# A second transformer mixer rearranged: half of its output projection among the last attention blocks, the first gate and value units early, the normalisation in pieces

## The chip, the cores and the metric

The kernel runs on one core of one Trainium2 chip. The metric is the device time of one execution in microseconds (us), lower is better. The core's engines are TensorE (PE in the profile, with its weight loads as PEld), VectorE (DVE), ScalarE (ACT), GpSimd (POOL) and SyncE (SP); each runs its own instruction list in order, and they wait for each other by semaphores.

## What is computed

Two networks of two layers each run one after the other on 512 tokens of width 1024. The change lies in the mixer of the second network, which runs once in each of its layers, between two feed-forward blocks. Cut to what matters:

```python
def hybrid_mixer(x, w_in, sc_conv_w, attn_sink, cc_conv_w, cc_conv_b, cc_ln_g, cc_ln_b, w_out):
    z = x @ w_in
    sc_b, sc_c, sc_h, q, k, v, cc_a, cc_gate = jnp.split(z, IN_OFFSETS, axis=-1)
    y_sc = sc_b * depthwise_conv(sc_c * sc_h, sc_conv_w)                      # 3 taps, 256 channels
    q, k = rope(q), rope(k)                                                   # 8 query heads, 2 key heads
    y_att = banded_window_attention(q, k, v, attn_sink)                       # blocks of 128, width 512
    u = depthwise_conv(cc_a * jax.nn.sigmoid(cc_gate), cc_conv_w) + cc_conv_b # 31 taps, 256 channels
    y_cc = jax.nn.silu(layer_norm(u, cc_ln_g, cc_ln_b))
    return jnp.concatenate([y_sc, y_att, y_cc], axis=-1) @ w_out

x = layer_norm(ALPHA * x + hybrid_mixer(x, ...), ln2_g, ln2_b)   # then the second feed-forward block
```

## The kernel before

One Python class stands for each engine (`TensorE`, `VectorE`, `ScalarE`, `Pool`, `Sync`) and writes that engine's whole instruction list. The classes walk through the same stages with the same generators, so the order on each engine is written out by hand; a `wait_ge` on a key waits for the instruction of another engine that announced the key.

**Precision.** A product of two fp32 matrices is made of three matmuls (`three`): high part by high part, high by low, low by high. Each weight unit is a 128x1024 fp32 tile. SP loads it to `raw` (three slots), ScalarE casts it to the high part `whi` (L2010), and VectorE subtracts to get the low part `wlo` (L1147). `whi` and `wlo` have four slots (`RING`), and a slot is free again when TensorE has announced `used` for the unit in it. `take()` and `ahead()` say where in the lists of ScalarE and VectorE the split of a coming unit stands; `spend(i)` marks a slot that may be taken.

**The mixer.** TensorE first makes the queries (four units, all held), then keys and values (`kv`, two units held, 96 matmuls of 256 columns). VectorE turns them with `rope_q` and `rope_k`, TensorE transposes them, ScalarE copies the transposes. Then come two interleaved streams. The main one, `attention`, goes through eight blocks (`BLOCKS`: four query blocks by two key heads): `scores` (four steps, a 256 or 384 column matmul each; VectorE adds the mask and finds the maximum; ScalarE's `weights` takes the exponential), then, for the block before, `values` (five steps: transposes of the weights on TensorE, ScalarE's copy `prT`, matmuls with `v` at L1134, and VectorE's scaling `ao`), then one empty step. That makes 80 steps. After every second block a transpose of the heads' outputs, `turn_ao`, is copied to `xh8` (ScalarE) and its low part to `xl8` (VectorE).

The other stream, `beside`, has 80 side steps of three 512-column matmuls, 8 steps to a unit: gate, value, gate, value (`conv_units`, for the 31-tap convolution), then two times three units for the 3-tap one (`short_conv`). Next to it stands `wide_conv`: on VectorE the 60 taps of the 31-tap convolution, one instruction of 512 columns each (two more instructions start the halves); on TensorE the two means of its normalisation, in banks of `ps`. A counter in `beside` sets its pace: no tap before side step 17, then four taps in three side steps up to tap 60, then one piece of the normalisation each fourth side step; `drain(wide)` runs what is left. `mix(..., 76, 74)` puts the two streams together, almost one to one, after six side steps. The end of the normalisation, one instruction list on VectorE (reciprocal at L1933, scaling, low part) and on ScalarE (`Silu`, cast), stands inside the last third of the stream.

After both streams `project` makes the output projection: two column halves, each four units (`w_out`) by four token tiles. For half 0 the units go one after another, for half 1 all four are held and the tiles follow each other (`late` is 1 and 4). VectorE adds the residual (`xn`, L1153) and does the layer norm tile by tile; TensorE transposes the first two tiles (`to_hT_tile`) inside half 1. Half 0 uses PSUM banks 4 to 7 and half 1 banks 0 to 3; the next feed-forward block begins with four units in banks 0 to 3.

**PSUM banks.** Eight banks, in rotations: `ps` is 4 to 7 (scores, transposes), `main2` is 0 and 1 (`kv`, `ao`), `side2` is 2 and 3 (side units). `bank()` waits until the last user of the bank is done.

Of the kernel before, what the change touches and what calls it, by code (L numbers as in the profile page):

```python
# [516 lines left out]
class TensorE(Lane):  # L517
    serial = False

    def __init__(self, k, e, name):  # L520
        super().__init__(k, e, name)
        self.all4, self.ps = Rota([0, 1, 2, 3]), Rota([4, 5, 6, 7])
        self.main2, self.side2 = Rota([0, 1]), Rota([2, 3])
        self.side3, self.adas = Rota([0, 1, 2]), Rota([3])
        self.pool3, self.small3 = Rota([2, 3, 7]), Rota([4, 5, 6])
# [67 lines left out]
    def tiles(self, keys, name, index, k0s, col, xh, xl, ready, rota, late):  # L593


        banks = [self.bank(rota, key) for key in keys]
        nk, held = 2 * len(k0s), []
        for ui, k0 in enumerate(k0s):
            held.append((ui,) + self.coming(name, index, n_pieces(k0, col)))
            if 0 <= len(k0s) - late <= ui < len(k0s) - 1:  # L600
                continue
            if ui == len(k0s) - 1:
                order = [(h, j, t) for t in range(4) for h in held for j in range(2)]
            else:
                order = [(h, j, t) for h in held for j in range(2) for t in range(4)]
            for q, ((u, wh, wl, i), j, t) in enumerate(order):
                k = 2 * u + j
                x = slice(k * 512 + t * 128, k * 512 + (t + 1) * 128)
                self.wait_ge(("hi", i), ("lo", i), *ready(k))
# [10 lines left out]
    def to_hT_tile(self, st, t):  # L620
        k = self.k
        self.wait_ge(("x", st, t), ("ident",))
        x = k.xs if st[0] == "A" else k.xn
        for d4 in range(2):
            bank = self.bank(self.ps, ("hT", st, t, d4))
            self.turn(bank, [x[:, t * 1024 + d * 128:t * 1024 + (d + 1) * 128] for d in range(4 * d4, 4 * d4 + 4)],
                      ("hT", st, t, d4))
# [374 lines left out]
    def mixer(self, l):  # L1002
# [5 lines left out]
        for t in range(4):  # L1008
            bank = self.bank(self.all4, ("q", l, t))
            for u, (wh, wl, i) in enumerate(units):  # L1010
                self.wait_ge(("hi", i), ("lo", i), ("hh", st, t, u // 2), ("hl", st, t, u // 2))
                for j in range(2):
                    d = 2 * u + j
                    x = slice(512 * d + 128 * t, 512 * d + 128 * t + 128)
                    a = self.three(bank[:, :], k.hh[:, x], k.hl[:, x], HALF(wh, j), HALF(wl, j), d == 0, d == 7)
                a.then_inc(*self.up(*([("used", i)] if t == 3 else []), *([("q", l, t)] if u == 3 else [])))
            if t < 2:
                self.to_hT_tile(st, 2 + t)
            else:
                self.turn_q(l, t - 2)  # L1020
        units = [self.coming("w_in_2", (l,), tuple((512 * u + 128 * j, 1280, 256) for j in range(4))) for u in range(2)]
        for t in range(4):
# [10 lines left out]
            if t % 2:  # L1033
                self.turn_q(l, 2 + t // 2)
        side = self.beside(l, 1)
# [4 lines left out]
        mix(self.attention(l), side, 76, 74)  # L1040
        drain(side)
        self.project("w_out_2", l, [0, 256, 512, 768], k.xh8, k.xl8, lambda d: (("xh", l, d), ("xl", l, d)), st, ("ffn2", l))
# [13 lines left out]
    def conv_units(self, l):  # L1056
        for j in range(2):
            yield from self.proj2(("cgt", l, j), l, 1792 + j * 128, self.side2)
            yield from self.proj2(("ca", l, j), l, 1536 + j * 128, self.side2)
        yield from self.short_conv(l)  # L1060
# [7 lines left out]
    def wide_conv(self, l):  # L1068
# [3 lines left out]
        bank = self.bank(self.ps, ("cm", l))  # L1072
# [5 lines left out]
        bank = self.bank(self.ps, ("cv", l))  # L1078
# [6 lines left out]
    def attention(self, l):  # L1085
        held = None
        for at in BLOCKS:
            yield from self.scores(l, *at)
            if held:
                yield from self.values(l, *held)  # L1090
            held = at
            yield
        yield from self.values(l, *held)
        self.turn_ao(l, 3)

    def turn_ao(self, l, nb):
        k = self.k
        bank = self.bank(self.ps, ("aot", l, nb))
        self.wait_ge(("aon", l, nb, 1))
        self.turn(bank, [k.ao[:, i * 128:(i + 1) * 128] for i in range(4)], ("aot", l, nb))  # L1100

    def scores(self, l, nb, kvh, k0, nk):
        k = self.k
        for i in range(4):
            h, q = 4 * kvh + i, 64 * kvh
            bank = self.bank(self.ps, ("as", l, nb, h))
# [7 lines left out]
    def values(self, l, nb, kvh, k0, nk):  # L1114
# [3 lines left out]
        out = self.bank(self.main2, ("ao", at))  # L1118

        def turned(i):  # L1120
            bank = self.bank(self.ps, ("at", at, i))
# [21 lines left out]
class VectorE(Lane):  # L1143
    at_steps = (2, 6)

# [628 lines left out]
    def project(self, n, st, nxt, s, ln, eps):  # L1774
        k = self.k
        self.at(("pj", st))
        stat = k.stat
        for half in range(2):
            late = (1, 4)[half]
            for ui in range(n):  # L1780
# [4 lines left out]
            for t in range(4):  # L1785
                if half and t == 2 and nxt != ("ffn1", DEPTH):
                    self.turn(nxt, 0)
                if t == 3:
                    self.spend(first + 1 if half else first)
# [32 lines left out]
    def mixer(self, l):  # L1822
# [12 lines left out]
        self.rope_q(l, 3)  # L1835
        used = [self.take() for _ in range(2)]
        self.rope_k(l, 0)
        for i in used:
            self.spend(i)
            self.ahead()  # L1840
# [4 lines left out]
        mix(self.attention(l), side, 76, 74)  # L1845
        drain(side)
        self.project(4, st, ("ffn2", l), ALPHA, "ln2", 1e-5)
# [31 lines left out]
    def conv_units(self, l):  # L1879
        k = self.k  # L1880
        z = [x[:, :] for x in k.t3]
        cp = k.ccp[:, :].rearrange("p (j n) -> p j n", j=2)
        for j in range(2):
            yield from self.steps()
            yield from self.steps()
            self.wait_ge(("cgs", l, j), ("ca", l, j), ("pads", l))
            self.tt(cp[:, j, 15:527], k.bank(("ca", l, j))[:, :], z[0], ALU.mult).then_inc(
                *self.up(("cuu", l, j), ("free", ("ca", l, j))))
        yield from self.short_conv(l)

    def short_conv(self, l):
# [3 lines left out]
        for j in range(2):  # L1895
            yield from self.steps()
# [4 lines left out]
            self.wait_ge()  # L1901
            self.ts(z[1], sp[:, j, 0:512], k.col(("sc", l, 0), j), None, ALU.mult).then_inc(*self.up())
            for w in (1, 2):
                self.wait_ge()
                self.stt(z[1], sp[:, j, w:w + 512], k.col(("sc", l, w), j), z[1], ALU.mult, ALU.add).then_inc(*self.up())
            yield from self.steps()
            self.wait_ge(("sc", l, j, 2))
            self.tt(z[1], z[1], k.bank(("sc", l, j, 2))[:, :], ALU.mult).then_inc(*self.up(("scy", l, j), ("free", ("sc", l, j, 2))))
            self.lower(HALF(k.xl8, j), z[1], HALF(k.xh8, j), [("xh", l, j)], [("xl", l, j)])

    def wide_conv(self, l):
# [21 lines left out]
        self.e.reciprocal(z[:, 0:512], z[:, 0:512]).then_inc(*self.up())  # L1933
        for j in range(2):
# [3 lines left out]
            self.lower(HALF(k.xl8, 6 + j), ac, HALF(k.xh8, 6 + j), [("xh", l, 6 + j)], [("xl", l, 6 + j)])  # L1938
# [62 lines left out]
class ScalarE(Lane):  # L2001
    at_steps = (0, 4)

# [353 lines left out]
    def project(self, n, st, nxt):  # L2357
        self.at(("pj", st))
        for half in range(2):
# [12 lines left out]
    def mixer(self, l):  # L2372
# [11 lines left out]
        for i in used[2:]:  # L2384
            self.spend(i)
            self.ahead()
        used = [self.take() for _ in range(2)]
        self.turned_q(l, 2)
# [4 lines left out]
        self.turned_q(l, 3)  # L2393
        self.value(l, 1)
        side = self.beside(l)
# [4 lines left out]
        mix(self.attention(l), side, 76, 74)  # L2400
        drain(side)
        self.project(4, st, ("ffn2", l))
# [21 lines left out]
    def conv_units(self, l):  # L2424
        k = self.k
        z = [x[:, :] for x in k.t3]
        for j in range(2):
            yield from self.steps()
            key = ("cgt", l, j)
            self.wait_ge(key, *([("cuu", l, 0)] if j else []))  # L2430
            self.act(z[0], k.bank(key)[:, :], ACT.Sigmoid).then_inc(*self.up(("cgs", l, j), ("free", key)))
            yield from self.steps()
        yield from self.short_conv(l)
# [14 lines left out]
    def wide_conv(self, l):  # L2448
# [10 lines left out]
        for j in range(2):  # L2459
# [4 lines left out]
            self.e.copy(HALF(k.xh8, 6 + j), ac).then_inc(*self.up(("xh", l, 6 + j)))  # L2464

# [333 lines left out]
```

## Time and profile before

| | us |
|---|---|
| median of 3 runs | 3529.51 (3528.66 to 3537.89) |
| the profiled execution, its own time | 3529.57 |
| its span, first to last instruction | 3527.7 |
| TensorE busy | 3347.5 (95%) |
| VectorE busy | 1724.9 (49%) |
| ScalarE busy | 1102.4 (31%) |
| mean granted TensorE clock | 0.975 |

The span is 1.9 us shorter than the execution's own time. Busy time of TensorE counts overlapping matmuls once; a matmul's end is modelled, so its start-to-start distance says more than its duration. The two mixers lie at about 1920 to 2175 us and 2920 to 3155 us of the span.

### The profile page before, as it was taken

The page shows a single profiled execution, that of the slowest core. Times are in us where ns is not written, and L with a number is a line of the kernel's source. Part 1 is how long each engine was busy: PE and PEld are TensorE (multiplying, and loading weights), DVE is VectorE, ACT ScalarE, POOL GpSimd, SP SyncE. Part 2 cuts the span into 40 slices and gives each one's busy share as a digit, 9 for nine tenths or more (in the row PEclk, how much of TensorE's full clock was granted, in tenths as well). Part 3 has the DMA queues.
Part 4 walks back from the last instruction along what each step waited for, and adds up shares of the span by engine and source line. Part 5 has one row for each costly group of instructions (what it writes and reads, how often), then busy time and mean ns, then how long its engine had stood idle before and what let it go on. Part 6 is the DMA issues. An engine that isn't in the chain of part 4 may idle for free. (4 is left out here: it accounts for less than half of the span.)

```text
span 3527.7 us, 42459 instructions
## 1 busy us (share of the span) xinstructions
PE 3347.5 (95%) x16776; PEld 2733.4 (77%) x16776; DVE 1724.9 (49%) x2524; ACT 1102.4 (31%) x1619; POOL 146.6 (4%) x204
## 2 busy tenths in 40 slices
PE   6999899989999999999999989999999999889999
PEld 5777777867777778788887758888888886578887
DVE  6655654456545544453334675332533346753334
ACT  4342223224432232233322443332233224323321
POOL 1000000001000000000001001000000000010000
PEclk9999999999999999999999989999999999899999
DMA  5222122132221111223232202223222322113232
GB/s 222 72 88 92 66 66 78 60 111 96 84 78 66 60 43 55 84 82 103 97 112 85 72 30 79 101 96 114 84 97 100 108 78 84 36 66 102 98 111 78
DMA packets 83494, 303.13 MB, mean 86 GB/s; under 512 B 9680, under 2 KB 9952, under 8 KB 83296
## 3 DMA queue, kind: packets, MB, share of 16 engines
q1 hardware_dynamic: 78064, 283.11, 23.5%
q0 software_dynamic: 5232, 17.31, 1.5%
q8 instruction: 133, 2.18, 0.2%
q14 instruction: 65, 0.53, 0.0%
HBM read 295.66 MB, written 4.72 MB: 85 GB/s over the span
## 5 line engine op out<-in xcount | busy, mean ns | idle before, releaser
L554 PE MATMUL bank<-hh,whi 128*128 128x512 f32 (+1 forms) x2704 | 1081.1, 400 | 25.0 <-DVE xn L1153 9.5
L556 PE MATMUL bank<-hh,wlo 128*128 128x512 f32 (+1 forms) x2704 | 1035.1, 383 | 0.0
L555 PE MATMUL bank<-hl,whi 128*128 128x512 f32 (+1 forms) x2704 | 1033.4, 382 | 0.0
L1147 DVE TENSOR_TENSOR wlo<-raw,whi 128x1024 fp32r<-128x1024 f32 x498 | 610.5, 1226 | 784.6 <-ACT whi L2010 722.6
L2010 ACT CAST whi<-raw 128x1024 fp32r<-128x1024 f32 x498 | 523.6, 1051 | 754.6 <-PE bank L556 696.4
L554 PEld LDWEIGHTS bank<-hh,whi 128*128 128x128 f32 x2704 | 520.0, 192 | 156.3 <-issue 46.6
L556 PEld LDWEIGHTS bank<-hh,wlo 128*128 128x128 f32 x2704 | 518.4, 192 | 98.7
L555 PEld LDWEIGHTS bank<-hl,whi 128*128 128x128 f32 x2704 | 520.6, 193 | 80.7 <-issue 2.7
L554 PE MATMUL bank<-whi,fh 128*128 128x512 f32 x704 | 274.4, 390 | 0.0
L556 PE MATMUL bank<-whi,fl 128*128 128x512 f32 x704 | 273.9, 389 | 0.0
L555 PE MATMUL bank<-wlo,fh 128*128 128x512 f32 x704 | 273.9, 389 | 0.0
L1147 DVE TENSOR_TENSOR tmp<-tmp,bank 128x512 f32<-128x512 f32 x104 | 71.5, 688 | 243.2 <-PE bank L556 240.9
L2354 ACT CAST fh<-tmp 128x512 fp32r<-128x512 f32 x88 | 54.5, 619 | 375.3 <-DVE tmp L1147 375.3
L555 PEld LDWEIGHTS bank<-wlo,fh 128*128 128x128 f32 x704 | 132.2, 188 | 27.3
L556 PEld LDWEIGHTS bank<-whi,fl 128*128 128x128 f32 x704 | 132.2, 188 | 27.3
L554 PEld LDWEIGHTS bank<-whi,fh 128*128 128x128 f32 x704 | 132.2, 188 | 27.3
L872 PEld LDWEIGHTS bank<-X,G 128*128 128x128 f32 x768 | 100.3, 195 | 27.9 <-ACT X L2273 14.0
L872 PEld LDWEIGHTS bank<-U,Y 128*128 128x128 f32 x768 | 100.1, 194 | 15.3 <-ACT Y L2277 8.6
L872 PE MATMUL bank<-X,G 128*128 128x64 f32 x768 | 101.0, 275 | 10.0 <-ACT X L2273 9.8
L1625 DVE COPY_PREDICATED U<-lmask,bank 128x256 f32<-128x256 uint32 x64 | 32.7, 510 | 149.3 <-PE bank L872 148.9
L872 PE MATMUL bank<-U,Y 128*128 128x64 f32 x768 | 98.9, 272 | 1.9 <-ACT Y L2277 1.9
L1147 DVE TENSOR_TENSOR fl<-tmp,fh 128x512 fp32r<-128x512 f32 x88 | 61.0, 693 | 71.6 <-ACT fh L2354 71.6
(320 smaller groups left out, 3707.8 us busy)
## 6 DMA issues: line engine op xcount, KB each, us to landing
raw<-in_W SPq DMA_DIRECT2D x514, 512.0 KB, 3.3
bc<-in_ln_g POOLq DMA_DIRECT2D x6, 512.0 KB, 4.3
bc<-in_ln_b POOLq DMA_DIRECT2D x6, 512.0 KB, 5.7
xn<-in_x SPq DMA_DIRECT2D x4, 512.0 KB, 8.9
mrg<-in_W SPq DMA_DIRECT2D x2, 1024.0 KB, 12.9
AR<-in_W SPq DMA_DIRECT2D x2, 1024.0 KB, 18.0
xn<-in_x POOLq DMA_DIRECT2D x4, 512.0 KB, 5.3
xd<-xn POOLq DMA_DIRECT2D x4, 512.0 KB, 3.5
```

The source lines that it names most:

```text
L554: e.matmul(out, ah, bh, start=first, stop=False, skip_group_check=True)
L555: e.matmul(out, ah, bl, start=False, stop=False, skip_group_check=True)
L556: return e.matmul(out, al, bh, start=False, stop=last, skip_group_check=True)
L872: t = self.e.matmul(bank[:, i * 64:(i + 1) * 64], lhs(i), rhs(i), start=True, stop=True, skip_group_check=True)
L1147: return self.e.tensor_tensor(o, a, b, op)
L1625: e.copy_predicated(FOUR_PART(U, 1, n), m, TIGHT(wb, n)).then_inc(*self.up(("cu", at, lv + 1), ("free", ("cw", at, lv))))
L2010: self.e.copy(self.k.halves(i)[0], self.k.raw_unit(n)).then_inc(*self.up(("hi", i)))
L2354: self.e.copy(HALF(k.fh, m), tm).then_inc(*self.up(("fh", st, m)))
```

## The change

1. The first gate and value units (`conv_pair(l, 0)`) come before `kv`. The first 10 taps run on VectorE around `rope_k(0)`, before `beside`.
2. In `beside` taps run one to a side step up to tap 60 at side step 50; each engine then has its own list of side steps at which it does a piece of the normalisation (`norm_steps`). The reciprocal is cut into two halves, and the scaling and the low part into separate pieces.
3. `out_half` makes half 0 of the output projection as 32 more side steps, in the row order `OUT_ROWS`: short convolution, wide convolution, then the two units of attention held together, tile by tile. With the 16 steps moved ahead the side stream has 96; `mix(..., 80, 78)` puts 78 beside attention after six, and 12 follow it.
4. PSUM banks: `ao` has bank 0 alone, the means bank 1, scores and transposes three banks (4, 5, 6) from the seventh block on; half 0 goes to 1, 7, 2, 3 and half 1 to 0, 4, 5, 6; the transposes of the first two tiles after it to 7, 1, 2, 3.
5. In `short_conv` the three tap instructions are spread over the unit's steps, and the low part is taken later (`low_short`).
6. `project` skips half 0's units; the mark `("pj", st)`, after which POOL loads the gain and bias rows of the layer norm (`bc`), stands before the mix.

```diff
+OUT_ROWS = (0, 768, 256, 512)
...
-    def beside(self, l, early=0):
-        wide = self.wide_conv(l)
-        done = 0
-        for n, _ in enumerate(self.conv_units(l), 1):
-            m = n + early
-            while done < min(60, (m - 17) * 4 // 3) + max(0, (m - 62) // 4):
-                next(wide, None)
-                done += 1
-            yield
-        drain(wide)
+    def taps(self, n):
+        for _ in range(n):
+            next(self.wide, None)
+    def beside(self, l):
+        done = 10
+        for m, _ in enumerate(itertools.chain(self.conv_units(l), self.out_half(l)), 1):
+            want = min(10 + m, 60) + sum(m >= x for x in self.norm_steps)
+            self.taps(want - done)
+            done = max(done, want)
+            yield
...
+    norm_steps = (52, 58)                     # TensorE
+    norm_steps = (54, 60, 63, 64, 66, 71)     # VectorE
+    norm_steps = (55, 61, 68)                 # ScalarE
...
+        self.ao1, self.ps3, self.norm1 = Rota([0]), Rota([4, 5, 6]), Rota([1])
+        self.first4, self.last4, self.spare4 = Rota([1, 7, 2, 3]), Rota([0, 4, 5, 6]), Rota([7, 1, 2, 3])
...
+    def out_half(self, l):                    # TensorE
+        k, st = self.k, ("mix", l)
+        self.mark(("hlast", ("ffn2", l)))
+        units, banks = [], []
+        for u, k0 in enumerate(OUT_ROWS):
+            units.append(self.coming("w_out_2", (l,), n_pieces(k0, 0)))
+            if u == 2:
+                continue
+            held = range(2, 4) if u == 3 else (u,)
+            order = [(t, v, j) for t in range(4) for v in held for j in range(2)]
+            for t, v, j in order if u == 3 else [(t, u, j) for j in range(2) for t in range(4)]:
+                wh, wl, i = units[v]
+                d = OUT_ROWS[v] // 128 + j
+                if v == j == 0:
+                    banks.append(self.bank(self.first4, ("pj", st, 0, t)))
+                x = slice(512 * d + 128 * t, 512 * d + 128 * t + 128)
+                self.wait_ge(("hi", i), ("lo", i), *([("xah", l, t), ("free", ("aot", l, t))] if u == 3 else [("xh", l, d), ("xl", l, d)]))
+                a = self.three(banks[t][:, :], k.xh8[:, x], k.xl8[:, x], HALF(wh, j), HALF(wl, j), v == j == 0, v == 3 and j == 1)
...
+                yield
...
         self.rope_q(l, 3)                     # VectorE, mixer
+        drain(self.conv_pair(l, 0))
+        self.wide = self.wide_conv(l)
+        self.taps(5)
         used = [self.take() for _ in range(2)]
         self.rope_k(l, 0)
+        self.taps(5)
...
-        self.e.reciprocal(z[:, 0:512], z[:, 0:512]).then_inc(*self.up())
+        self.e.reciprocal(z[:, 0:256], z[:, 0:256]).then_inc(*self.up())
+        yield
+        self.e.reciprocal(z[:, 256:512], z[:, 256:512]).then_inc(*self.up())
+        yield
...
-        mix(self.attention(l), side, 76, 74)
+        self.at(("pj", st))
+        mix(self.attention(l), side, 80, 78)
         drain(side)
-        self.project(4, st, ("ffn2", l), ALPHA, "ln2", 1e-5)
+        self.project(4, st, ("ffn2", l), ALPHA, "ln2", 1e-5, self.held)
```

## Rows read from the trace of the kernel before

**Rows 1.** The page: TensorE's line, and the two groups that split weight units.

```profile
PE 3347.5 (95%) x16776; PEld 2733.4 (77%) x16776; DVE 1724.9 (49%) x2524; ACT 1102.4 (31%) x1619; POOL 146.6 (4%) x204
...
L1147 DVE TENSOR_TENSOR wlo<-raw,whi 128x1024 fp32r<-128x1024 f32 x498 | 610.5, 1226 | 784.6 <-ACT whi L2010 722.6
L2010 ACT CAST whi<-raw 128x1024 fp32r<-128x1024 f32 x498 | 523.6, 1051 | 754.6 <-PE bank L556 696.4
```

**Rows 2.** Busy time by stretches: length, engines' busy (instructions), clock, DMA share, GB/s.

```profile
1960.71:2148.70 187.99, 164.61 (x777) 120.65 (x776) 121.30 (x234) 76.61 (x151) 1.06 (x2) 0.91 0.18 59
2940.32:3128.30 187.98, 164.65 (x777) 120.66 (x776) 121.29 (x234) 76.63 (x151) 1.06 (x2) 0.91 0.17 59
2940.32:2953.05 12.73, 12.73 (x109) 12.72 (x108) 6.42 (x12) 4.78 (x7) 0.00 (x0) 1.00 0.47 162
2953.05:2958.03 4.98, 4.84 (x26) 3.77 (x24) 3.62 (x6) 2.36 (x5) 0.00 (x0) 1.00 0.55 166
2976.00:3060.20 84.20, 76.20 (x326) 51.53 (x325) 73.86 (x139) 32.91 (x72) 0.00 (x0) 0.90 0.11 38
3078.70:3091.00 12.30, 0.03 (x2) 0.01 (x1) 7.68 (x10) 4.94 (x8) 0.00 (x0) 0.59 0.12 43
3091.00:3106.46 15.46, 13.05 (x64) 10.92 (x64) 3.21 (x11) 7.06 (x18) 0.00 (x0) 0.77 0.00 1
3106.46:3128.30 21.84, 21.84 (x96) 18.11 (x97) 8.75 (x10) 4.84 (x5) 1.06 (x2) 1.00 0.44 143
```

**Rows 3.** TensorE's waits, 2930 to 3170: us in total, times, longest.

```profile
PE bank L1134 <- ACT prT L2511: 13.3, 3, 12.3
PE bank L560 <- DVE sm L1968: 3.3, 2, 2.8
```

**Rows 4.** VectorE's groups from 2976.00 to 3060.20, shapes apart.

```profile
L1153 DVE SCALAR_TENSOR_TENSOR acc<-ccp,cols,acc 128x512 f32<-128x512 f32 x60 | 45.1, 752 | 2.1
...
L1984 DVE RECIPROCAL sm<-sm 128x4 f32<-128x4 f32 x5 | 0.9, 178 | 0.2
```

**Rows 5.** Timeline of the normalisation's end: start, duration, engine, line, operation, idle before.

```profile
3079.99 3.35 DVE L1933 RECIPROCAL zc<-zc 128x512 f32<-128x512 f32 x1
...
3084.21 1.28 ACT L2005 ACT_TABLE_LOAD   x1 [8.90 <-DVE acc L1153]
3085.51 0.72 ACT L2005 ACTIVATE acc<-acc,cols 128x512 f32<-128x512 f32 x1
...
3090.03 0.69 DVE L1147 TENSOR_TENSOR xl<-acc,xh 128x512 fp32r<-128x512 f32 x1 [1.57 <-ACT xh L2464]
...
3091.00 0.48 PE L1134 MATMUL bank<-v,prT 128*128 128x64 f32 x1 [12.27 <-ACT prT L2511]
```

**Rows 6.** Timeline, TensorE: starts of scores, side steps beside values, and a mean.

```profile
2958.03 0.67 PE L1108 MATMUL bank<-kT,qT 64*128 64x256 f32 x2
...
2959.53 0.70 PE L1108 MATMUL bank<-kT,qT 64*128 64x256 f32 x2
...
3012.98 0.48 PE L554 MATMUL bank<-hh,whi 128*128 128x512 f32 x1
...
3014.34 0.48 PE L554 MATMUL bank<-hh,whi 128*128 128x512 f32 x1
...
3015.91 0.91 PE L1108 MATMUL bank<-kT,qT 64*128 64x384 f32 x2
...
3017.64 0.91 PE L1108 MATMUL bank<-kT,qT 64*128 64x384 f32 x2
...
3060.70 1.98 PE L1075 MATMUL bank<-acc,mean 128*128 128x512 f32 x4 [0.80 <-DVE sm L1968]
```

**Rows 7.** Timeline of the seam to the next feed-forward block.

```profile
3149.06 1.42 DVE L1147 TENSOR_TENSOR hl<-bank,hh 128x512 fp32r<-128x512 f32 x2
...
3150.56 1.23 DVE L1147 TENSOR_TENSOR wlo<-raw,whi 128x1024 fp32r<-128x1024 f32 x1
...
3155.25 0.36 PE L554 MATMUL bank<-hh,whi 128*128 128x256 f32 x1 [3.18 <-DVE xn L1153]
```

More of the change, by code:

```diff
@@ L1032, in mixer @@
                 a.then_inc(*self.up(*([("used", i)] if t == 3 else []), *([("kv", l, t // 2)] if u and t % 2 else [])))
-            if t % 2:
-                self.turn_q(l, 2 + t // 2)
-        side = self.beside(l, 1)
+        self.wide = self.wide_conv(l)
+        self.taps(10)
+        side = self.beside(l)
         for n in range(6):
@@ L1039, in mixer @@
                 self.turn_k(l, n // 3)
-        mix(self.attention(l), side, 76, 74)
+        self.at(("pj", st))
+        mix(self.attention(l), side, 80, 78)
         drain(side)
-        self.project("w_out_2", l, [0, 256, 512, 768], k.xh8, k.xl8, lambda d: (("xh", l, d), ("xl", l, d)), st, ("ffn2", l))
+        keys = [("pj", st, 1, t) for t in range(4)]
+        for n, _ in enumerate(self.tiles(keys, "w_out_2", (l,), OUT_ROWS, 512, k.xh8, k.xl8, lambda d: (), self.last4, 4)):
+            if n in (9, 11):
+                self.to_hT_tile(("ffn2", l), n // 11, self.spare4)
+        self.all4.n = 0
+    def out_half(self, l):
[16 more added lines that the diff above has]
+                a = self.three(banks[t][:, :], k.xh8[:, x], k.xl8[:, x], HALF(wh, j), HALF(wl, j), v == j == 0, v == 3 and j == 1)
+                done = [("pj", st, 0, t)] if v == 3 and j else []
+                if t == 3 and j:
+                    done.append(("used", i))
+                if done:
+                    a.then_inc(*self.up(*done))
+                yield
     def turn_q(self, l, t):
@@ L1054, in turn_k, with conv_pair @@
         self.turn(bank, [k.kn[a][:, n * 128:(n + 1) * 128] for n in range(2)], ("kt", l, a))
[L1056 to L1060, printed above, removed]
+    def conv_pair(self, l, j):
+        yield from self.proj2(("cgt", l, j), l, 1792 + j * 128, self.side2)
+        yield from self.proj2(("ca", l, j), l, 1536 + j * 128, self.side2)
     def short_conv(self, l):
@@ L1071, in wide_conv @@
             yield
-        bank = self.bank(self.ps, ("cm", l))
+        bank = self.bank(self.norm1, ("cm", l))
         self.wait_ge(("acc", l), ("mean", l))
@@ L1077, in wide_conv @@
         yield
-        bank = self.bank(self.ps, ("cv", l))
+        bank = self.bank(self.norm1, ("cv", l))
         self.wait_ge(("csq", l))
@@ L1086, in attention @@
         held = None
-        for at in BLOCKS:
+        self.rows_rota = self.ps
+        for n, at in enumerate(BLOCKS):
+            if n == 6:
+                self.rows_rota = self.ps3
             yield from self.scores(l, *at)
@@ L1097, in turn_ao @@
         k = self.k
-        bank = self.bank(self.ps, ("aot", l, nb))
+        bank = self.bank(self.rows_rota, ("aot", l, nb))
         self.wait_ge(("aon", l, nb, 1))
@@ L1117, in values @@
         n0 = 4 * (2 * nb + kvh)
-        out = self.bank(self.main2, ("ao", at))
+        out = self.bank(self.ao1, ("ao", at))
         def turned(i):
-            bank = self.bank(self.ps, ("at", at, i))
+            bank = self.bank(self.rows_rota, ("at", at, i))
             self.wait_ge(("ap", at, i), ("ident",))
@@ L1772, in ffn, with project @@
         self.project(11, st, nxt, 2 * ALPHA, ln, eps)
-    def project(self, n, st, nxt, s, ln, eps):
+    def project(self, n, st, nxt, s, ln, eps, held=()):
         k = self.k
-        self.at(("pj", st))
+        if not held:
+            self.at(("pj", st))
         stat = k.stat
@@ L1779, in project @@
             late = (1, 4)[half]
-            for ui in range(n):
+            for ui in range(0 if held and not half else n):
                 i = self.take()
@@ L1788, in project @@
                 if t == 3:
-                    self.spend(first + 1 if half else first)
+                    for i in (first + 1,) if half else held or (first,):
+                        self.spend(i)
                     self.ahead()
@@ L1844, in mixer @@
             next(side)
-        mix(self.attention(l), side, 76, 74)
+        self.at(("pj", st))
+        mix(self.attention(l), side, 80, 78)
         drain(side)
-        self.project(4, st, ("ffn2", l), ALPHA, "ln2", 1e-5)
+        self.project(4, st, ("ffn2", l), ALPHA, "ln2", 1e-5, self.held)
     def turned_by(self, o, tm, x, cs, sn):
@@ L1877, in rope_k, with conv_pair, out_half @@
         self.tt(o, o, tm, ALU.add).then_inc(*self.up(("kn", l, a)))
-    def conv_units(self, l):
+    def conv_pair(self, l, j):
         k = self.k
-        z = [x[:, :] for x in k.t3]
         cp = k.ccp[:, :].rearrange("p (j n) -> p j n", j=2)
[L1883 to L1889, printed above, removed]
+        yield from self.steps()
+        yield from self.steps()
+        self.wait_ge(("cgs", l, j), ("ca", l, j), ("pads", l))
+        self.tt(cp[:, j, 15:527], k.bank(("ca", l, j))[:, :], k.t3[0][:, :], ALU.mult).then_inc(
+            *self.up(("cuu", l, j), ("free", ("ca", l, j))))
+    def out_half(self, l):
+        for n, _ in enumerate(self.steps(), 1):
+            if n == 2:
+                self.low_short(l, 1)
+            yield
+        yield from self.steps()
+        self.held = self.take(), self.take()
+        for _ in range(16):
+            yield
     def short_conv(self, l):
@@ L1895, in short_conv @@
         for j in range(2):
-            yield from self.steps()
+            for n, _ in enumerate(self.steps(), 1):
+                if j and n == 2:
+                    self.low_short(l, 0)
+                yield
             yield from self.steps()
@@ L1937, in wide_conv @@
             self.stt(ac, ac, k.col(("cc_lg", l), j), z[:, 0:512], ALU.mult, ALU.mult).then_inc(*self.up(("ccn", l, j)))
-            self.lower(HALF(k.xl8, 6 + j), ac, HALF(k.xh8, 6 + j), [("xh", l, 6 + j)], [("xl", l, 6 + j)])
+        yield
+        for j in range(2):
+            self.lower(HALF(k.xl8, 6 + j), HALF(k.acc, j), HALF(k.xh8, 6 + j), [("xh", l, 6 + j)], [("xl", l, 6 + j)])
     def attention(self, l):
@@ L2355, in ffn, with project @@
         self.project(11, st, nxt)
-    def project(self, n, st, nxt):
-        self.at(("pj", st))
-        for half in range(2):
+    def project(self, n, st, nxt, held=()):
+        if not held:
+            self.at(("pj", st))
+        for i in held:
+            self.spend(i)
+        for half in range(1 if held else 0, 2):
             late = (1, 4)[half]
@@ L2386, in mixer @@
             self.ahead()
+        for n, _ in enumerate(self.conv_pair(l, 0), 1):
+            if n == 9:
+                self.turned_q(l, 2)
+        self.turned_q(l, 3)
         used = [self.take() for _ in range(2)]
-        self.turned_q(l, 2)
         self.value(l, 0)
@@ L2392, in mixer @@
             self.ahead()
-        self.turned_q(l, 3)
         self.value(l, 1)
+        self.wide = self.wide_conv(l)
+        self.taps(10)
         side = self.beside(l)
@@ L2399, in mixer @@
                 self.turned_k(l, n // 3)
-        mix(self.attention(l), side, 76, 74)
+        self.at(("pj", st))
+        mix(self.attention(l), side, 80, 78)
         drain(side)
-        self.project(4, st, ("ffn2", l))
+        self.project(4, st, ("ffn2", l), self.held)
     def turned_q(self, l, t):
@@ L2422, in value, with conv_pair, out_half @@
                     k.bank(key)[:, :].rearrange("p (t c n) -> p t c n", t=2, c=2)[:, :, 1, :]).then_inc(*self.up(("vv", l, a), ("free", key)))
-    def conv_units(self, l):
+    def conv_pair(self, l, j):
         k = self.k
[L2426 to L2433, printed above, removed]
+        key = ("cgt", l, j)
+        yield from self.steps()
+        self.wait_ge(key, *([("cuu", l, 0)] if j else []))
+        self.act(k.t3[0][:, :], k.bank(key)[:, :], ACT.Sigmoid).then_inc(*self.up(("cgs", l, j), ("free", key)))
+        yield from self.steps()
+    def out_half(self, l):
+        yield from self.steps()
+        yield from self.steps()
+        self.held = self.take(), self.take()
+        for _ in range(16):
+            yield
     def short_conv(self, l):
@@ L2464, in wide_conv @@
             self.e.copy(HALF(k.xh8, 6 + j), ac).then_inc(*self.up(("xh", l, 6 + j)))
+        yield
     def attention(self, l):
```

35 lines of the change are left out of this document (24 added, 11 removed).

## The prediction

> **What bounds the kernel now.** I read the page first: TensorE is busy 95% of the span [rows 1], so over the whole kernel only its waits and its slow clock can be won, unless work is removed, and the change removes none. Next, the busy time by stretches around the two mixers. From the transposes before `kv` to the end of output half 0 takes 187.98 us, and 187.99 us in the first mixer [rows 2], so what holds for one counts twice. TensorE is busy only 164.65 us of these, at a clock of 0.91: this is the weakest place in the kernel, and the reader should see two causes in its parts.
>
> First, from 2976.00 to 3060.20, while the 60 taps run, VectorE is busy 73.86 of 84.20 us in 139 instructions; between them is a small gap each, so it is nearly full, and it sets the pace. TensorE waits for it in places (3.3 us for score banks, 2.8 the longest) [rows 3] and its clock is 0.90. Second, from 3078.70 to 3091.00 TensorE does nothing at all. The wait list names `prT`, 12.3 us at once [rows 3]; the timeline shows why the copy is late: ScalarE and VectorE stand in the end of the normalisation (reciprocal 3.35 us, `Silu` after an idle 8.90 us, last low part at 3090.03), and the copy is behind it in ScalarE's list [rows 5]. The clock in this stretch is 0.59 and in the 15.46 us after it 0.77 [rows 2], where 1 is the 2.4 GHz level and 0.5 the 1.2 GHz level: of those 15.46 us, 46% ran at half clock, so about 3.6 us were lost besides the wait.
>
> **The change, summed for one mixer.** I lay the new order out from the same start (2940.32) to the start of half 1.
>
> (a) Gate and value units of pair 0, 48 matmuls. Half 0 gives the price: 96 matmuls in 21.84 us [rows 2], 0.228 each, so 11.0 us. A side step of three is 0.68.
>
> (b) `kv` and its transposes, as now: 12.7 us [rows 2].
>
> (c) Six side steps and the key transposes, as now 5.0 us [rows 2]. New in VectorE's list ahead of `rope_k(1)` are 10 taps (7.5 us) [rows 4]; TensorE's `turn_k(1)`, and everything behind it, waits for `rope_k(1)`. Counting the list from the end of (a) (convolution input, five taps, a unit's low part at 1.23 [rows 1], `rope_k(0)`, five taps, two low parts, `rope_k(1)`), I get about 17.5 us, against 16.3 for TensorE: 1.4 us of new wait with the semaphore.
>
> (d) Side steps 7 to 50, with 50 taps instead of 60. By TensorE: 8 scores of 256 columns at 1.50 a step and 12 of 384 at 1.73 [rows 6], together 32.8; value steps at 1.36 for three key blocks [rows 6] and an estimated 1.13 for two (two thirds of what is over 0.68), 8 each, 19.9; 44 transposes, 6.0 (from (b): 12.73 less 96 matmuls at half of 0.228, over the 13 other instructions, 0.14 each [rows 2]); 8 steps without any of these, 5.5. Sum 64. By VectorE: today's 84.20 less 11 instructions at 0.75 [rows 4] is 75.9, less one step of its other work, 0.9: 75. The larger one decides, so I take 75; 64 is the lower bound. The upper bound is today's 84.
>
> (e) Side steps 51 to 84. VectorE has no taps left here, so I count TensorE: 4 scores at 1.73 and 8 at 1.50, 18.9; value steps 8 at 1.36 and 8 at 1.13, 19.9; 48 transposes 6.6; 6 bare steps 4.1; two means at 1.98 or less [rows 6], 3.8. Sum 53. For small waits, as [rows 3] has them outside the longest ones (1.0 and 0.5 us), I add 2; lower bound 0, upper bound the long wait and slow clock of today, which is a rival below.
>
> (f) The last 12 side steps, 8.2 us, with the last `turn_ao` 0.5 and its wait for `ao`, as now about 0.6. They cover the copy and the low part of the last attention tile, which only the last three matmul steps need. Sum 9.2.
>
> Together 11.0 + 12.7 + 6.4 + 75 + 55 + 9.2 = 169.3, against 187.98: **18.7 us less**. Put the other way: 12.3 of the wait and 3.6 of slow clock go, and the rest comes from VectorE's stage and the seam into the projection.
>
> (g) After half 1, TensorE's first feed-forward matmul waits 3.18 us for the residual addition of tile 3, because that frees the fourth bank [rows 7]. With the new banks those four are freed by the transposes' readers instead, done at 3150.48 (3149.06 + 1.42) [rows 7]. What is late next is the first unit's low part at 3151.79 (3150.56 + 1.23) [rows 7], just when half 1 ends. Gain 3.2, lower bound 0 if a later unit waits anyway.
>
> **Costed at nothing.** The split reciprocal: a four-column one takes 0.18 [rows 4] and the whole 3.35 [rows 5], so two halves cost 3.35 plus about 0.18; it lies in (e), where VectorE has room (without taps it had 73.86 less 45.1, 28.8 us, in the 45 steps of the tap stage [rows 2, 4]). If that cover were gone, 0.2 us. The early `bc` loads move 1 MB while the DMA share is 0.17 [rows 2]; if they collided, three raw slots stand between. Half 1 needs all four units in a tile's order, and the splits of its last two cannot begin before the held units are used: cast 1.05 and subtraction 1.23 [rows 1] end about 1.3 and 2.6 us after half 0, and TensorE asks for them 2.7 and 4.1 us after it. Without that cover each would cost its 1.05 to 2.3 us. One bank for `ao`: TensorE's `values` waits until VectorE has scaled the block before; five or six steps lie between, except before the last block, where one empty step of 0.68 stands against 0.42 and a semaphore. Three row banks: at a step of 1.5 us each is read before its turn.
>
> **A rule beside the rows.** In [rows 5] the switch of ScalarE's function table takes 1.28 us and the `Silu` starts 0.02 later. The Trainium skill (ScalarE: Activation LUTs, "What ACT_TABLE_LOAD costs") adds a drain of about 1.38 us to each switch, 2.66 in all, which speaks against putting `Silu` between two exponentials: an estimate by that page adds 2.8 us a mixer for two switches: nothing if hidden, otherwise 3491.4 instead of 3485.8. The rows go against the drain, so I keep 1.28.
>
> **Total.** (18.7 + 3.2) x 2 = 43.8 us. The profiled execution took 3529.57 (span 3527.7 and 1.9 around it), the median is 3529.51. 3529.6 - 43.8 = **3485.8**, some 1.2% less.
>
> **Rivals.**
> *TensorE sets the pace everywhere* (VectorE's 256-column scores in the first blocks are cheaper than those of today's stage, and the clock stays full). (d) is 64 and no wait is added: 154.4, 36.8 less with the seam, 3456. Against it: VectorE has 73.86 less 8.3, 65.6 busy us, and the gaps between some 130 instructions.
> *VectorE's stage doesn't shrink*: in-order waits eat what ten taps free, (d) stays 84: 3485.8 + 18 = 3504. For it: of the 84.20 now 10.3 are gaps and waits [rows 2].
> *The chain is only moved.* TensorE now wants both low parts of the wide convolution at side step 73, VectorE gives them at 71 and ScalarE's `Silu` comes at 68; from the reciprocal at 63 there are ten steps, some 15 us, while today this end lasts 10.7 (3079.99 to 3090.72) [rows 5]. If ScalarE is late by its exponentials, wait and slow clock come back: 15.9 x 2 more, 3518.
> *Slower: the single bank 0.* Every `values` would wait for VectorE's `ao` of the block before, which stands behind taps and low parts in its list. Seven waits in each mixer; from 3.1 us each (43.8/14) the gain is gone; at 5 us each the time is 3556. Against it: with one bank more, TensorE's longest waits today are for others [rows 3], and VectorE has five steps of time.
> *It does nothing on balance*: smaller waits eat it, 3530.
>
> **Chances.** Forecast 0.52 (own range 3475 to 3497); TensorE everywhere 0.14; stage not shrunk 0.16; chain moved 0.10; slower 0.04; nothing 0.04. The range 3456 to 3516 leaves out half of the second case, half of the chain's, and the last two: some 0.2. A measurement here tells about 0.3%, 10.6 us, from no change. Faster by more: the first three cases and most of the fourth, 0.90; within: the rest of the fourth and most of the last, 0.06; slower 0.04.
>
> **What would show it.** No TensorE wait above 3 us in either mixer. From the transposes before `kv` to the first half 1 matmul about 169 us. The tap stage about 75 us with VectorE nearly full, the 34 steps after it some 55 with TensorE full at clock 1.0. The reciprocal as two instructions of about 1.8. The first feed-forward matmul right behind half 1. The prediction is wrong if TensorE waits at the first `out_half` steps of unit 768 (for `xl`), at L1134 before the last block, or if VectorE shows idle time in the tap stage while TensorE waits too.

## The result and the profile after

The changed kernel takes 3490.13 us (median of 4 runs, 3487.3 to 3499.98) against 3529.33 for the kernel before (4 runs): ratio 0.9886, 95% interval 0.9867 to 0.9905, 39 us less. I had forecast 3486 in a range of 3456 to 3516. In a later session the same kernel took 3486.99 against 3529.84 (0.9881, 0.9864 to 0.9899).

The page after: TensorE's line and the span (compare [rows 1]; TensorE does the same 16776 matmuls).

```profile
span 3485.5 us, 42457 instructions
...
PE 3327.7 (95%) x16776; PEld 2715.6 (78%) x16776; DVE 1725.2 (49%) x2526; ACT 1098.4 (32%) x1615; POOL 146.8 (4%) x204
```

Busy time by stretches in the second mixer: from the transposes ahead of the first pair to the first matmul of half 1; the tap stage (first score to last tap); from there to the last `turn_ao`; and two parts of the latter. Columns as in [rows 2].

```profile
2917.86:3090.56 172.70, 159.86 (x777) 116.65 (x776) 121.88 (x236) 74.15 (x149) 1.06 (x2) 0.96 0.18 61
2948.59:3024.30 75.71, 71.62 (x306) 47.34 (x306) 65.79 (x131) 32.01 (x74) 1.06 (x2) 0.93 0.17 57
3024.30:3081.87 57.57, 50.55 (x253) 36.68 (x253) 29.08 (x66) 29.31 (x59) 0.00 (x0) 0.97 0.11 38
3062.90:3067.69 4.79, 0.34 (x3) 0.10 (x2) 2.86 (x8) 2.44 (x6) 0.00 (x0) 1.00 0.15 44
3067.69:3081.87 14.18, 13.59 (x76) 11.92 (x77) 2.73 (x7) 6.28 (x17) 0.00 (x0) 0.88 0.14 49
```

The first line answers to the second of [rows 2]: the same 777 matmuls, 172.70 us in place of 187.98, and the clock 0.96 in place of 0.91. The tap stage is 75.71, with 65.79 busy in 131 instructions on VectorE. The fourth line is what stayed wrong: 4.8 us with next to nothing on TensorE.

TensorE's waits, 2900 to 3170 (compare [rows 3]).

```profile
PE bank L570 <- DVE xl L1194: 6.1, 3, 4.5
PE bank L1180 <- ACT prT L2600: 2.3, 3, 1.3
PE bank L570 <- DVE sm L2042: 1.9, 1, 1.9
PE bank L564 <- DVE qn L1194: 1.1, 1, 1.1
```

The 12.3 us of [rows 3] are gone, and so is the 3.2 at the seam. Two waits are new: 4.5 us for a low part (`xl`) and 1.1 for the rotated queries (`qn`). (`sm` are VectorE's small values for the softmax, maxima and sums; the score bank is free when VectorE has read it for them.) Timeline around the first:

```profile
3055.23 1.28 ACT L2080 ACT_TABLE_LOAD   x1 [1.93 <-DVE acc L1200]
...
3059.33 1.28 ACT L2080 ACT_TABLE_LOAD   x1
...
3060.13 0.66 PE L570 MATMUL bank<-ident,ao 128*128 128x128 f32 x4
...
3063.45 1.04 ACT L2085 CAST whi<-raw 128x1024 fp32r<-128x1024 f32 x1
3064.52 0.59 ACT L2575 CAST xh<-bank 128x512 fp32r<-128x512 f32 x1
3064.62 1.23 DVE L1194 TENSOR_TENSOR wlo<-raw,whi 128x1024 fp32r<-128x1024 f32 x1 [3.58 <-ACT whi L2085]
...
3066.94 0.69 DVE L1194 TENSOR_TENSOR xl<-bank,xh 128x512 fp32r<-128x512 f32 x1
3067.69 0.41 PE L570 MATMUL bank<-ident,pr 128*128 128x128 f32 x1 [4.45 <-DVE xl L1194]
```

Read it from the end. TensorE wants a bank for a transpose of attention weights. With three banks in turn, the next one is that of `turn_ao`, written at 3060.13 and read last at 3067.63. ScalarE's copy of it comes only at 3064.52, because in ScalarE's list it stands behind the normalisation's `Silu`, two table switches, four exponentials and a weight cast. VectorE adds its part: it idles 3.58 us for that weight cast, then makes the weight's low part, a mask and three small values for the softmax first, and so reads the bank (`xl`, 3066.94) only 1.83 us after ScalarE's copy is done (3065.11).

The seam to the feed-forward block, timeline (compare [rows 7]): it starts right behind half 1's last matmul.

```profile
3113.89 0.39 PE L566 MATMUL bank<-whi,xl 128*128 128x512 f32 x1
...
3114.16 0.36 PE L564 MATMUL bank<-hh,whi 128*128 128x256 f32 x1
```

### The profile page after: what moved, and what is told of

Its sections match the earlier page's. It is cut to its first block and busy times, and to the rows that moved or that the text cites. A ratio compares the mean times of both kernels' runs of the same rounds, so it can differ in the third digit from the quotient of the medians.

```text
span 3485.5 us, 42457 instructions
## 1 busy us (share of the span) xinstructions
PE 3327.7 (95%) x16776; PEld 2715.6 (78%) x16776; DVE 1725.2 (49%) x2526; ACT 1098.4 (32%) x1615; POOL 146.8 (4%) x204
```

## Experiments

Whole times of one kernel differ by up to 0.5% between runs, and part of that lies where no edit is (last section). So beside the medians I give the length of the mixer, read the same way from every timeline: start of the second query tile's transposes to the first feed-forward matmul. It is 214.9 us before in both mixers. Tap stage means first score to last tap, from start to start.

| kernel | median us (runs) | ratio to before, 95% | mixers, us | tap stages, us |
|---|---|---|---|---|
| before | 3529.33 (4) | | 214.9, 214.9 | 101.4, 101.4 |
| changed | 3490.13 (4) | 0.9886, 0.9867 to 0.9905 | 196.6, 196.3 | 74.0, 74.9 |
| changed, again | 3486.99 (4) | 0.9881, 0.9864 to 0.9899 | 197.4, 194.6 | 75.6, 72.2 |
| half 0 back | 3518.33 (9) | 0.9960, 0.9944 to 0.9976 | 208.2, 210.6 | 74.0, 75.5 |
| seam banks | 3517.17 (10) | 0.9954, 0.9938 to 0.9971 | 205.9, 204.8 | 75.6, 74.9 |
| no early taps | 3507.19 (4) | 0.9930, 0.9907 to 0.9953 | 204.2, 206.1 | 82.5, 83.4 |
| chain whole | 3497.74 (4) | 0.9900, 0.9876 to 0.9924 | 200.4, 199.5 | 75.6, 74.8 |
| tile 3 in bank 0 | 3503.55 (4) | 0.9920, 0.9900 to 0.9939 | 199.9, 199.4 | 74.0, 73.8 |
| Silu later | 3486.48 (4) | 0.9882, 0.9866 to 0.9898 | 194.3, 192.2 | 74.0, 73.8 |
| no switch | 3478.0 (1) | | 193.1, 189.4 | 74.0, 72.2 |
| fewer taps | 3474.74 (1) | | 189.2, 188.9 | 66.5, 66.4 |
| Silu later, pair in banks 0 and 1 | 3482.21 (4) | 0.9868, 0.9853 to 0.9883 | 192.6, 192.7 | 74.1, 74.2 |
| the same, slower taps | 3486.74 (4) | 0.9869, 0.9853 to 0.9884 | 193.9, 192.5 | 79.3, 77.8 |

(The tap stage before is longer than the 84.20 of [rows 2] because it is taken from the first score.) The lengths come from one profiled execution of each kernel, the medians from all its runs. The changed kernel's four mixer lengths lie 2.8 us apart, so differences under that need an average and a wait in the trace to stand.

**Half 0 back.**

```diff
     def out_half(self, l):                    # the same on every engine
-        ... (the 32 steps of half 0)
+        for _ in range(32):
+            yield
...
+        self.project("w_out_2", l, [0, 256, 512, 768], k.xh8, k.xl8, ...)   # both halves, old banks
```

> The changed kernel with part 3 alone undone: half 0 of the output projection is made after attention again, unit by unit, in banks 4 to 7, and half 1 in banks 0 to 3; the 32 side steps are left empty, so that taps and normalisation keep their steps. Theory A (half 0 covers the waits of the last attention blocks and the way into the projection): the last 20 attention steps stand bare, some 5 to 8 us of waits and slow clock a mixer, plus 2.1 us ahead of the projection and 3.2 at the seam, so 10 to 14 a mixer: 3510 to 3518 against 3490. Theory B (the early pair, the pace of the taps and the pieces of the normalisation bring it all, and half 0 only changes places): only the seam comes back, 3.2 a mixer: 3496.

(The mark for the `bc` loads goes back behind the mix with it.) The mixers are 11.6 and 14.3 us longer than the changed kernel's, 13.0 in the mean. The bare stretch of attention and its clock (busy times, 3049.00 to 3089.05), and two of TensorE's waits that the changed kernel does not have:

```profile
3049.00:3089.05 40.05, 30.48 (x138) 22.33 (x137) 20.57 (x49) 22.93 (x52) 0.00 (x0) 0.72 0.04 14
```

```profile
PE bank L564 <- DVE xn L1175: 3.2, 1, 3.2
PE bank L1129 <- DVE sm L2012: 2.2, 1, 2.2
```

Theory A holds: without side steps the last attention blocks leave TensorE busy 30.5 of 40 us, at a clock of 0.72. Moving the 96 matmuls of half 0 (21.84 us) is worth 13.0 us a mixer with the seam, some 9.8 without. The wait of 4.45 us is 2.37 here, so a part of it comes with the moved half.

**Seam banks.**

```diff
-        ... self.last4 ... Rota([0, 4, 5, 6]) ...
+        ... self.last4 ... Rota([0, 1, 2, 3]) ...
-                self.to_hT_tile(("ffn2", l), n // 11, self.spare4)
+                self.to_hT_tile(("ffn2", l), n // 11)
```

> The changed kernel with half 1 in banks 0 to 3 again and the first two transposed tiles in the rotation 4 to 7. Theory A (the fourth bank is what TensorE waited for at the seam): a wait of about 3.2 us for the residual addition comes back before the first feed-forward matmul in both mixers, 3496 against 3490. Theory B (the low part of the first units is what counts there): no wait above 0.5 us, 3490.

The seam's wait came back as A has it, but I had missed a second one: half 1 takes its four banks at its start, and banks 1, 2 and 3 then still hold half 0. TensorE's timeline, start of half 1 and seam:

```profile
3106.24 0.47 PE L564 MATMUL bank<-whi,xh 128*128 128x512 f32 x1 [3.45 <-DVE xn L1200]
...
3134.83 0.55 PE L564 MATMUL bank<-hh,whi 128*128 128x256 f32 x1 [3.18 <-DVE xn L1200]
```

So 8.9 us a mixer belong to both waits and what follows them, and the experiment did not isolate what it was made for. The next one does.

**Tile 3 in bank 0.**

```diff
-        ... self.last4 ... Rota([0, 4, 5, 6]) ...
+        ... self.last4 ... Rota([4, 5, 6, 0]) ...
```

> The changed kernel with half 1 of the output projection in banks 4, 5, 6, 0 in place of 0, 4, 5, 6: nothing else moves, only tile 3 now stands in bank 0, which the next feed-forward block takes first. Theory A (that block waits for the bank of tile 3): a wait of 3.2 us for the residual addition before its first matmul, 3 to 4.5 us a mixer with the clock, 3494 to 3499 against 3488. Theory B (the split of the first units sets its start): a wait under 0.5 us and no difference.

```profile
3123.81 0.58 PE L564 MATMUL bank<-hh,whi 128*128 128x256 f32 x1 [3.12 <-DVE xn L1200]
```

The wait is back (3.48 in the first mixer, 3.12 in the second), and the mixers are 3.2 us longer in the mean (199.6 against 196.5): theory A. The median rose by 13 us and not by the 6 to 11 expected. The profiled executions differ by 12.1 (3499.39 and 3487.3); 6.3 of these are in the mixers, the others outside.

**No early taps.**

```diff
-        done = 10
+        done = 0
-            want = min(10 + m, 60) + ...
+            want = min(max(0, (m - 6) * 15 // 11), 60) + ...
-        self.taps(5)          # twice, and taps(10) on the other engines
```

> The changed kernel without the ten early taps: all 60 taps stand in side steps 7 to 50, 15 taps to 11 steps. Theory A (VectorE sets the pace while the taps run): the stretch from the first score to the last tap grows from 75.7 us to 83 or 84, the stretch before it shrinks by up to 1: 6 to 8 us a mixer, 3502 to 3506. Theory B (TensorE's own work and its clock set it): at most 2 us a mixer, 3490 to 3494.

The tap stages grow to 82.5 and 83.4, the mixers by 8.7 in the mean, a little more than the 6 to 8 expected. VectorE is busy 74.77 us in the stage (busy times, to the first mean):

```profile
2956.48:3040.60 84.12, 74.66 (x306) 48.51 (x306) 74.77 (x143) 31.96 (x74) 1.09 (x2) 0.90 0.16 55
```

**Fewer taps.**

```diff
             for w in range(1, 31):
+                if 11 <= w <= 20:
+                    yield
+                    continue
                 self.wait_ge()
```

> The changed kernel with 20 of the 60 taps of the wide convolution left out (taps 11 to 20 of either half; their places in the list stay empty). Theory A (VectorE paces the tap stage): from the first score to the last tap 75 us become what TensorE's work asks, 63 to 66. Theory B (TensorE's matmuls, with the clock that they get, pace it already): 72 or more.

The same from the other side. The stage is 66.4, TensorE has no wait above 0.5 us in it and its clock is full:

```profile
2943.41:3010.53 67.12, 66.65 (x306) 43.90 (x306) 51.70 (x112) 31.96 (x74) 1.06 (x2) 1.00 0.19 63
```

Both hold theory A: in the changed kernel VectorE still paces the taps; TensorE alone would need 66.4, 2 more than my count of 64.

**Chain whole.**

```diff
-        self.e.reciprocal(z[:, 0:256], z[:, 0:256]).then_inc(*self.up())
-        yield
-        self.e.reciprocal(z[:, 256:512], z[:, 256:512]).then_inc(*self.up())
-        yield
+        self.e.reciprocal(z[:, 0:512], z[:, 0:512]).then_inc(*self.up())
...
-    norm_steps = (54, 60, 63, 64, 66, 71)     # VectorE
+    norm_steps = (54, 60, 63)
-    norm_steps = (55, 61, 68)                 # ScalarE
+    norm_steps = (55, 61, 64)
```

> The changed kernel with the end of the normalisation in one piece: on VectorE the whole reciprocal, both scalings and both low parts at side step 63, on ScalarE both Silu with their casts at step 64. Theory A (the pieces keep the copies and low parts of others from standing behind the chain): TensorE waits 6 to 12 us once in each mixer, with slow clock behind it, 3504 to 3520. Theory B (half 0's matmuls now cover the chain anyway): 3488 to 3493.

```profile
PE bank L1180 <- ACT prT L2595: 8.4, 3, 7.3
PE bank L570 <- DVE xl L1194: 2.5, 3, 0.9
```

The wait for `prT` of [rows 3] is back at L1180, 7.3 us instead of 12.3. But it takes the place of the 4.45 and 1.3 us waits of the changed kernel (the longest for `xl` is now 0.9), so only 3.5 us a mixer are lost. The wait lies in A's 6 to 12, the time of 3497.74 between the two theories, below A's 3504 and above B's 3493: pieces help, but much less than I thought, since in pieces the chain has a wait of its own.

**Silu later.**

```diff
-    norm_steps = (54, 60, 63, 64, 66, 71)     # VectorE
+    norm_steps = (54, 60, 63, 64, 66, 72)
-    norm_steps = (55, 61, 68)                 # ScalarE
+    norm_steps = (55, 61, 71)
```

> The changed kernel with ScalarE's last piece of the normalisation (table switch, two Silu with casts) at side step 71 in place of 68, behind the exponentials of the seventh block and not ahead of them, and VectorE's last low parts at 72 in place of 71. Theory A (the 4.4 us wait at the last value steps comes from ScalarE's list, where Silu, two table switches and four exponentials stand in a row ahead of the copy of the heads' outputs): the wait falls to 2 us or less, with under 1 us new at side step 73, so 2 to 4 us a mixer: 3483 to 3487 against 3490. Theory B (three row banks are too few, whatever ScalarE does): the wait stays above 3.5 us and the time at 3490.

```profile
3064.29 0.44 PE L570 MATMUL bank<-ident,pr 128*128 128x128 f32 x2 [2.22 <-DVE xl L1194]
```

In both mixers 4.45 became 2.22, and no new wait stands at side step 73. The mixers are 3.2 us shorter in the mean than in the first profile of the changed kernel, 3.0 than its four lengths. So the wait speaks for theory A; the medians (3486.48 against 3486.99 in one session) do not show the gain.

**No switch.**

```diff
-            self.act(ac, ac, ACT.Silu, bias=k.col(("cc_lb", l), j)).then_inc(*self.up())
+            self.act(ac, ac, ACT.Square, bias=k.col(("cc_lb", l), j)).then_inc(*self.up())
-        self.act(z[:, 0:512], z[:, 0:512], ACT.Sqrt).then_inc(*self.up(("csd", l)))
+        self.act(z[:, 0:512], z[:, 0:512], ACT.Square).then_inc(*self.up(("csd", l)))
```

> The changed kernel with Square in place of both Silu and of Sqrt in the normalisation (another function, the same sizes and order), which needs no switch of ScalarE's tables. By the row of 1.28 us two switches stand ahead of the late copy, so the wait of 4.4 us falls by 2.6, to about 1.8. By the rule of the Trainium skill (ScalarE: Activation LUTs, What ACT_TABLE_LOAD costs) each switch costs 2.66, the two 5.3, and the wait would go altogether. If the banks alone are the cause, it stays at 4.4.

```profile
3060.05 0.44 PE L570 MATMUL bank<-ident,pr 128*128 128x128 f32 x2 [1.90 <-DVE xl L1194]
```

4.45 less 1.90 is 2.55, two switches at 1.28 (2.56). By the 2.66 of the Trainium skill (ScalarE: Activation LUTs, "What ACT_TABLE_LOAD costs") the wait would have gone altogether, so the trace does not agree with the drain here, and ScalarE's list is the cause of at least this part of the wait. What is left, about 2 us in both kernels, no experiment took apart. The trace points at VectorE's list: ScalarE's copy is done at 3057.47 (3056.88 + 0.59), and VectorE's low part of the same bank starts 1.83 us later, at 3059.30, behind a weight's low part and a mask. Another bank would have needed one that half 0 holds.

**Silu later, pair in banks 0 and 1.**

```diff
     def conv_pair(self, l, j):
-        yield from self.proj2(("cgt", l, j), l, 1792 + j * 128, self.side2)
-        yield from self.proj2(("ca", l, j), l, 1536 + j * 128, self.side2)
+        yield from self.proj2(("cgt", l, j), l, 1792 + j * 128, self.side2 if j else self.main2)
+        yield from self.proj2(("ca", l, j), l, 1536 + j * 128, self.side2 if j else self.main2)
```

> As the kernel with the later Silu, and the first gate and value units in PSUM banks 0 and 1, which are free, in place of 2 and 3, which the last query tiles still hold. Theory A (the new wait of 1.14 us for the rotation of the last query tile is a wait for its bank): it goes, 1.1 us a mixer more than the later Silu alone gives, 3480 to 3485. Theory B (the next wait in line takes its place, for the keys): no more than 0.3 a mixer.

The 1.14 us wait for `qn` is gone, and from the query transposes to the first score it is 29.4 us in place of 30.7: a wait for a bank, theory A. Over the whole mixer only 0.6 us more than with the later Silu alone are seen (192.7 against 193.2 in the mean), less than the scatter. 3482.21 is the lowest median of a complete kernel, 0.9868 of before; its interval (0.9853 to 0.9883) overlaps that of the changed kernel, while its mixers are 3.6 us shorter each (192.7 against 196.2, the mean of the changed kernel's four).

**Slower taps.**

```diff
-            want = min(10 + m, 60) + ...
+            want = min(10 + m - m // 12, 60) + ...
+    norm_steps = (55, 60)                     # TensorE
+    norm_steps = (57, 62, 65, 66, 68, 72)     # VectorE
+    norm_steps = (58, 63, 71)                 # ScalarE
```

> The kernel with the later Silu and the pair in banks 0 and 1, and 50 taps spread over side steps 7 to 54 in place of 7 to 50; the means come at 55 and 60, VectorE's pieces at 57, 62, 65, 66, 68 and 72, ScalarE's at 58, 63 and 71. Theory A (VectorE paces only where the taps are, and has time behind them): four steps of 1.55 us now hold taps that VectorE would otherwise do at full load, 2 to 3 us a mixer, 3475 to 3479 against 3482. Theory B (the end of the normalisation has no slack): TensorE waits at side step 73 and nothing is won or 2 to 4 us are lost.

```profile
3036.02 1.41 DVE L1194 TENSOR_TENSOR acc<-acc,bank 128x512 f32<-128x512 f32 x2
...
3037.52 1.06 ACT L2080 ACTIVATE zc<-acc 128x1024 f32<-128x1024 f32 x1 [3.42 <-DVE acc L1194]
3038.72 1.19 PE L1124 MATMUL bank<-zc,mean 128*128 128x512 f32 x1 [2.21 <-DVE tz L1200]
...
3062.06 0.47 PE L564 MATMUL bank<-whi,xh 128*128 128x512 f32 x1 [0.57 <-DVE xl L1194]
```

A miss: nothing won (193.2 against 192.7). Theory B was right that there is no slack, and TensorE does wait at side step 73, but only 0.57 us (and 0.50 at step 69); most is at another place, the second mean. The list names VectorE's `tz`; that is only the last to end, the mean needs ScalarE's square, which waited 3.42 us for VectorE's subtraction.

**Changed, again.**

> The changed kernel once more, on the chip and in the hour of the runs beside it: 3490 give or take 5 if it stands to the kernel before as in its first runs, with the same waits of 4.4 and 1.3 us in each mixer.

As expected: 3486.99, with waits of 4.45 and 1.29 us in both mixers.

## Why the prediction was right, step by step

Stretches of the second mixer, first from this profile, in brackets what I had.

- *(a) to (c)*, the pair, `kv` and six steps: 30.7 us from the query transposes to the first score (30.1). The sum was right, the wait in it was not: TensorE shows no wait for `rope_k(1)` at `turn_k(1)`; instead 1.14 us go for the bank of the last query tile, which the pair's value unit takes over. I had not asked which banks the moved units would find. The pair in banks 0 and 1 shows it.
- *(d)*, the tap stage: 75.7 (75). VectorE paces it, shown from both sides, and its busy time of 65.79 us is what the first rival reckoned (65.6). The ten early taps are worth 8.7 us (8.3 in the step from 84.2 to 75.9).
- *(e)*, steps 51 to 84: 57.6 (55). This term was mis-sized. I allowed 2 us for small waits and costed three row banks at nothing, since each score is read before its turn; but `turn_ao` also takes one of the three, and it was held 7.5 us (3060.13 to 3067.63), for which TensorE waited 4.45. In the whole stretch TensorE was idle 7.0 us (57.57 less 50.55) where I had allowed 2; its busy time, slow clock included, was 50.6 where I had counted 53. So my count of its work was too high, and that hid half of the missed waits: part of the closeness of this term is luck. The wait is the rival "the chain is only moved" in small, at another key: what was late was not the chain's own result but the copy behind `Silu` in ScalarE's list.
- *(f)*: 8.7 (9.2). The last 12 side steps cover the last tile; its wait for `ao` is 0.59 us as before.
- *(g)*, the seam: 3.2 us, shown by tile 3 in bank 0 (3.2 a mixer).

Of the signs that I had named, two failed with (e): a wait above 3 us stands in both mixers, and the clock of the stretch is 0.97, not 1.0. The others came: the reciprocal is two instructions of 1.75 us, the first feed-forward matmul follows half 1 at once, TensorE has no wait for `xl` at unit 768, and none at the values' matmuls (L1180, L1134 before) behind the 1.30 us at 3052.85.

The mixers became 18.3 and 18.6 us shorter (18.7 + 3.2 = 21.9 forecast), 36.9 together; the medians say 39 and the two profiled executions 42.3. What exceeds 36.9 lies outside the two mixers, where nothing was changed. So it is in part luck that the median comes as near to the forecast 43.8 as it does. The difference in the mixers, 3.4 us each, is mainly (e), 2.6 of it. The rivals: TensorE does not pace the tap stage, the stage did shrink, and the list of TensorE's waits has none ahead of `values` for the single `ao` bank, so the slower case had no ground. By undoing one part at a time, half 0 with its banks is worth 13.0 us a mixer, the early taps 8.7, the pieces 3.5. They sum to 25.2 and not to 18.5: they are not shares of the gain, since undoing one part changes the waits that the others leave, as the 4.45 us did in two of the three. What each part would bring alone to the kernel before was not run.

## What to carry to other kernels

When independent matmuls lie in a solid stretch after a stage full of waits, move them into it as filler; price the move by the waits and the slow clock of that stage, not by the length of the moved work (21.8 us moved, 13 gained). Before you do, list for each moved step which PSUM bank it takes over and who reads that bank last: the two waits that were new here and the one at the seam were all for banks. On an in-order engine ask not only when a moved piece is done but what now stands behind it.

## What the runs showed that I had not expected

- The time outside the edits varies. From the first seam to the second mixer's query transposes, 763.4 us in one execution of the changed kernel and 766.6 in another, 763.3 to 766.7 over all kernels (764.7 before). Changes of 3 to 4 us a mixer are seen only in the timeline of the mixer itself. I have not looked for the cause.
- The medians of two kernels lie higher than their mixers explain: seam banks by 27 us with 17.8 in the mixers, tile 3 in bank 0 by 13 with 6.3. For seam banks a part of this is that the mixers were read from one of its fastest executions (3509.01 of ten from 3507.69 to 3525.01, 21.7 above the changed kernel's profiled one). What is left stays open.
- The clock around a wait of that size is not the same each time. In the second mixer of the first profile the stretch of the 4.45 us wait itself had a granted clock of 1.00 and the 14.2 us after it 0.88, though TensorE was busy 13.6 of them; in the same wait of the kernel's second profile it was 0.87 and then 0.81. With the later Silu the wait is 2.22 us, and behind it the clock was 0.88 in the first mixer and 1.00 in the second. So I can't say that 4.45 us are what slowed the clock there. Only the long bare stretch is plain: with 30.5 of 40 us busy it was 0.72.
